# Trunk of retention, spatial gating and dilated attention: GpSimd's sums of weights begun earlier, probabilities and retention's output a tile later

## The chip, the cores and the metric

One core of a Trainium2 chip runs the whole program. TensorE (PE) multiplies, VectorE (DVE) and ScalarE (ACT) work on its results, GpSimd (POOL) and SyncE (SP) issue transfers; each engine works through its own list of instructions in order and waits on semaphores. The metric is the device time of one execution in microseconds; the median of three runs counts.

## What is computed

Two layers over 512 positions of width 1024. The reference, cut to what matters here:

```python
for l in range(DEPTH):                      # DEPTH = 2
    h = rms_norm(x, g_mix[l])
    z = h @ w_in[l]                         # q, k, v of all mixers and the branch gates
    # A: retention, 4 heads (rotation, decayed causal scores, head norm, swish gate)
    # B: spatial gating in chunks of 128
    # C: dilated attention, 4 heads x 3 groups; q and k are RMS-normalized per head
    for gi, (win, dil) in enumerate(((128, 1), (512, 4), (2048, 16))):
        o, lse = dilated_window_attention(qc[:, :, gi], kc[:, :, gi], vc[:, :, gi], win, dil)
    wts = jax.nn.softmax(jnp.stack(lses, axis=0), axis=0)   # weights of the three groups
    yc = jnp.sum(wts[..., None] * jnp.stack(outs, axis=0), axis=0)
    merged = (gt[:, :, 0] * (ya @ w_branch[l, 0])           # gt = sigmoid of the branch gates
              + gt[:, :, 1] * (yb @ w_branch[l, 1]) + gt[:, :, 2] * (yc @ w_branch[l, 2]))
    x = x + merged @ w_o[l]
    h = rms_norm(x, g_ffn[l])
    gate, up = jnp.split(h @ w_gate_up[l], 2, axis=-1)
    x = x + (silu(gate) * up) @ w_down[l]
```

## The kernel before

Everything is kept transposed, 128 channels by 512 positions. The weights come from DRAM in slabs of eight 128x128 blocks (512 KB): SP loads a slab into one of three `raw` buffers (L712), ACT rounds it to `w_high` (L1011, "split_high") and DVE takes the rest, `w_low` (L1215, "split_low"), into one of three places. A main tile is one output of 128 channels: eight blocks, three matmuls each (high by high, low by high, high by low), 24 matmuls of 512 columns. Its bank is evacuated by DVE, and the main tile after the next one takes that bank again.

`schedule()` writes one list of steps, and every engine walks the list and takes its part of each step. For each main tile the list has, in this order: the main matmuls; the high split of the slab that takes the place just used (so ACT waits there until PE has finished the tile); the steps in `pre` of that tile; the evacuation; the low split; the steps in `post`. So a step moved by one tile moves behind a whole main tile on PE, and behind another split on ACT.

The tiles of a head h of the attention are k0 k1 k2 q0 q1 q2 v0 v1 v2; after the fourth head come rq rk rv rg for each of retention's four heads, then the gates and projections of branch 2, and so on. The attention of a head is worked off beside the next head's projections (t is the number of the head's tile k0, so t + 9 is the next head's k0):

- `scores`, `expo`: scores in PSUM, DVE adds the mask and takes row maxima, ACT's exponentials with their sums (L1179).
- `gather`, `swap`: DVE writes the maxima and sums of own groups into `pairs` (L1477); SP sends them through DRAM and back (L750 to L760), so that each position meets its other order.
- `weigh`: DVE makes `shift` from own and exchanged pairs (L1483 to L1485), ACT takes `shift_exp` (L1184), DVE makes the factors and scales all probabilities (L1488 to L1500).
- `ptrans`: PE turns four units of probabilities (L949) into the two turn banks, 4 and 5, by turns; ACT copies them out (L1190). Every user of a turn bank (also `vtrans`, L931, and `rowstat`) waits until the user before the last has been copied or read.
- `pv`: values by probabilities, in bank 6. `high`/`low yc`: ACT and DVE split the result.
- For the next head at the same time: `square` and `split_sq` of k and q (L1101, L1108, L1430), `rowstat ck` (PE sums squares over channels with ones_r), `rowstd` (ACT's square root, L1117), `rowinv` (DVE's reciprocal, L1434), `rowscale`; `stat cq`, PE's column statistic of the squared q (`ones,sq`, eight matmuls of one column).
- Retention: `rotate`, `rscore`, `rpv`, `ocopy` of the output, the same square, statistic and reciprocal, `rowscale` and the split of yr.

An activation other than copy and square needs its table in ACT; where two in a row need different ones, the program has an ACT_TABLE_LOAD between them.

The feed-forward part multiplies seven products of quarters for nine of its eleven pairs of tiles ("quick"), and four of the seven need sums of weights, t1 to t4. POOL makes these in DRAM with eight transfers of 512 KB for each pair, four of them adding (L673, L675), each step waiting for the one before. It starts when tile rv0 of the layer has been stored. SP waits for a pair's eight before it loads its first sum.

Of the kernel before, what the change touches and what calls it, by code (L numbers as in the profile page):

```python
# [33 lines left out]
HEADS = 4  # L34
# [6 lines left out]
PAIRS = D_FF // P // 2  # L41
# [57 lines left out]
A11B11, S2T2, A12B21, S1T1, S3T3, S4B22, A22T4 = range(7)  # L99
# [4 lines left out]
AT = {t: i for i, t in enumerate(TILES)}  # L104
# [14 lines left out]
STRIDE = 16 * SLABS  # L119
# [74 lines left out]
def schedule():  # L194
    pre = {i: [] for i in range(len(TILES))}
    post = {i: [] for i in range(len(TILES))}
    for h in range(HEADS):
        t = AT["k", h, 0]
        for j in range(N_GROUP):

            post[t + j] += [("square", "ck", h, j), ("split_sq", "ck", h, j)]

            pre[t + (2, 4, 4)[j]] += [("rowstat", "ck", h, j), ("rowstd", "ck", h, j)]
            post[t + 3 + j] += [("rowinv", "ck", h, j), ("rowscale", "ck", h, j)]

            post[t + 3 + j] += [("square", "cq", h, j)]
            pre[t + 4 + j] += [("stat", "cq", h, j)]
            if j > 0:
                pre[t + 7 + j] += [("vtrans", "v", h, j)]
        pre[t + 6] += [("rstd", "cq", h)]  # L210
        pre[t + 7] += [("scores", h, 0), ("scores", h, 1), ("expo", h, 0), ("vtrans", "v", h, 0)]
        pre[t + 8] += [("scores", h, 2), ("scores", h, 3), ("expo", h, 1)]
        post[t + 8] += [("gather", h), ("swap", h)]
        if h < HEADS - 1:
            pre[t + 11] += [("weigh", h)]
        pre[t + 12] += [("ptrans", h, 0), ("ptrans", h, 1)]
        pre[t + 13] += [("ptrans", h, 2), ("pv", h, 0), ("ptrans", h, 3)]
        pre[t + 14] += [("pv", h, 1), ("pv", h, 2), ("high", "yc", h), ("low", "yc", h)]
    for h in range(HEADS):
        t = AT["rq", h]  # L220
        post[t] += [("rotate", "rq", h)]
        if h == 0:

            pre[t + 2] += [("weigh", HEADS - 1)]
        post[t + 1] += [("rotate", "rk", h)]
        pre[t + 3] += [("vtrans", "rv", h)] + [("rscore", h, m) for m in range(2)]
        pre[t + 4] += [("rscore", h, m) for m in range(2, BLK)]
        pre[t + 6] += [("rpv", h), ("ocopy", h), ("square", "r", h), ("split_sq", "r", h)]
        pre[t + 7] += [("rowstat", "r", h), ("rowstd", "r", h)]
        post[t + 7] += [("rowinv", "r", h)]  # L230
        post[t + 8] += [("rowscale", "r", h), ("high", "yr", h), ("low", "yr", h)]
    t = AT["sv", 0]
    for c in range(HEADS):
        pre[t + c + 1] += [("vtrans", "sv", c)]
# [64 lines left out]
STAT_AT, BCAST_AT = 3, 6  # L299
AFTER_NORM = (AT["k", 0, 0], AT["fgate", 0, 0])  # L300
STEPS = schedule()


# [46 lines left out]
def build(nc, x_in, weights, sums_dram, gain_first, vecs, spatial, rows, rotation, decay, masks, ident_in, pairs_dram, out):  # L350
    with ExitStack() as ctx:  # L351
# [3 lines left out]
        def signal(name, events, ahead=()):  # L355
            return Signal(ctx.enter_context(nc.semaphore(name)), events, ahead)
# [110 lines left out]
        tile_stored = signal("tile_stored", BY_VECTOR)  # L467
# [200 lines left out]
        def _(pool):  # L668
# [7 lines left out]
                started[0] += 1  # L676

            for layer in range(DEPTH):
                pool.wait_ge(tile_stored.sem, tile_stored.at(layer * STRIDE, AT["rv", 0]))
                for n, u in enumerate(QUICK_UNITS):  # L680
                    first = AT["quick", u, 0]
                    b11, b21, b22 = (weights[layer * HOST_ROWS + SOURCE[BLOCKS[first + step][0][0]]]
# [522 lines left out]
        def _(dve):  # L1205
# [26 lines left out]
            for base in range(0, DEPTH * STRIDE, STRIDE):  # L1232
# [23 lines left out]
                for kind, *key in STEPS:  # L1256
# [24 lines left out]
                    elif kind == "evac":  # L1281
# [41 lines left out]
                        elif t[0] in ("q", "k"):  # L1323
                            operands = by_phase(qk[t[2] + (3 if t[0] == "k" else 0)], src, norm_rstd[:, :], t[2] > 0)
                            dve.tensor_tensor(*operands, ALU.mult).then_inc(tile_stored.sem, 1)
                        elif t[0] == "proj":
                            _, br, n = t
                            dve.wait_ge(activated.sem, activated.at(base, AT["gate", br, n]))
                            g = gates[GATE_TILES.index(AT["gate", br, n]) % 2]
# [331 lines left out]
```

## Time and profile before

| what | value |
|---|---|
| median of three runs | 1927.08 us (1926.92 to 1927.63) |
| profiled execution, its own time | 1928.07 us |
| its span | 1926.3 us |
| PE busy | 1902.9 us |
| DVE busy | 1236.6 us |
| ACT busy | 854.4 us |
| POOL busy (issuing) | 97.0 us |
| TensorE's granted clock, mean | 0.999 |
| ACT_TABLE_LOADs (six lines together) | 49 |

The span is from the first instruction of the program to the last. PE's matmuls overlap in the records: a matmul of 512 columns is shown with 0.38 us, but starts 0.22 us after the one before it, so starts are to be compared, not ends. The time in brackets at the end of a row is idle time of its engine and what ended it.

### The profile page before, as it was taken

To read this page: it belongs to the slowest core of one execution; us is meant where nothing else is said; L and a number is where in the kernel's file an instruction comes from. 1 tells how busy PE (TensorE), PEld (TensorE's weight loads), DVE (VectorE), ACT (ScalarE), POOL (GpSimd) and SP (SyncE) were. 2 spreads that over 40 slices of the span, in tenths; PEclk is the share of its full clock that TensorE was granted. 3 is DMA by queue.
4 is the path that set the end of the run, shared out by engine and by line. 5 is a ranking of instruction groups with operands and counts; after the bars stand their busy time and mean duration, and the time that the engine had idled before them with its cause. 6 is when DMAs were issued, how large, how long until landed. Compare 5 with 4: busy or idle time off the path is not lost. (4 is left out here: it accounts for less than half of the span.)

```text
span 1926.3 us, 26698 instructions
## 1 busy us (share of the span) xinstructions
PE 1902.9 (99%) x10664; PEld 1703.1 (88%) x10664; DVE 1236.6 (64%) x1633; ACT 854.4 (44%) x1194; POOL 97.0 (5%) x148
## 2 busy tenths in 40 slices
PE   7999999999999999999999999999999999999999
PEld 6888888888888899899888888888888888998998
DVE  6666756745666787267576666677366667863775
ACT  5444444434234455255445444344343344542554
POOL 0000001111111000000000000011111110000000
PEclk9999999999999999999999999999999999999999
DMA  5322247777777356356333222577777773553663
GB/s 190 83 81 84 78 121 197 192 207 202 214 206 198 99 158 182 102 183 198 122 108 87 74 78 79 138 198 188 216 193 199 200 206 106 176 157 109 204 204 126
DMA packets 85897, 295.68 MB, mean 153 GB/s; under 512 B 20368, under 2 KB 20624, under 8 KB 84624
## 3 DMA queue, kind: packets, MB, share of 16 engines
q1 hardware_dynamic: 73104, 218.49, 36.4%
q0 software_dynamic: 12672, 75.51, 17.3%
q8 instruction: 85, 1.39, 0.3%
q14 instruction: 36, 0.29, 0.1%
HBM read 291.79 MB, written 77.66 MB: 192 GB/s over the span
## 5 line engine op out<-in xcount | busy, mean ns | idle before, releaser
L1011 ACT ACTIVATE w_high<-raw 128x1024 fp32r<-128x1024 f32 x396 | 418.1, 1056 | 813.3 <-PE bank L823 685.7
L823 PE MATMUL bank<-h_high,w_high 128*128 128x512 f32 x1472 | 570.1, 387 | 12.8 <-DVE h_low L1220 11.3
L1215 DVE TENSOR_TENSOR w_low<-raw,w_high 128x1024 fp32r<-128x1024 f32 x396 | 482.8, 1221 | 123.3 <-ACT w_high L1011 117.5
L823 PE MATMUL bank<-h_low,w_high 128*128 128x512 f32 x1472 | 559.2, 380 | 0.0
L823 PE MATMUL bank<-h_high,w_low 128*128 128x512 f32 x1472 | 559.1, 380 | 0.0
L823 PEld LDWEIGHTS bank<-h_high,w_high 128*128 128x128 f32 x1472 | 279.2, 190 | 55.9 <-issue 9.4
L823 PEld LDWEIGHTS bank<-h_high,w_low 128*128 128x128 f32 x1472 | 279.0, 190 | 39.8
L823 PEld LDWEIGHTS bank<-h_low,w_high 128*128 128x128 f32 x1472 | 279.2, 190 | 38.3
L823 PE MATMUL bank<-in_high,w_high 128*128 128x512 f32 x672 | 255.0, 379 | 0.0
L823 PE MATMUL bank<-in_low,w_high 128*128 128x512 f32 x672 | 254.7, 379 | 0.0
L823 PE MATMUL bank<-in_high,w_low 128*128 128x512 f32 x672 | 254.7, 379 | 0.0
L1322 DVE TENSOR_TENSOR scaled<-bank,norm_rstd 128x512 f32<-128x512 f32 x128 | 93.7, 732 | 108.3 <-PE bank L823 107.8
L841 PE MATMUL bank<-s_high,w_high 128*128 128x256 f32 x576 | 158.4, 275 | 0.0
L842 PE MATMUL bank<-s_low,w_high 128*128 128x256 f32 x576 | 158.4, 275 | 0.0
L843 PE MATMUL bank<-s_high,w_low 128*128 128x256 f32 x576 | 158.4, 275 | 0.0
L823 PEld LDWEIGHTS bank<-in_high,w_high 128*128 128x128 f32 x672 | 127.0, 189 | 18.3 <-DVE in_low L1413 0.4
L823 PEld LDWEIGHTS bank<-in_high,w_low 128*128 128x128 f32 x672 | 127.0, 189 | 18.0
L823 PEld LDWEIGHTS bank<-in_low,w_high 128*128 128x128 f32 x672 | 127.0, 189 | 17.8
L843 PEld LDWEIGHTS bank<-s_high,w_low 128*128 128x128 f32 x576 | 110.6, 192 | 0.0
L842 PEld LDWEIGHTS bank<-s_low,w_high 128*128 128x128 f32 x576 | 110.6, 192 | 0.0
L841 PEld LDWEIGHTS bank<-s_high,w_high 128*128 128x128 f32 x576 | 110.6, 192 | 0.0
L1345 DVE TENSOR_TENSOR xT<-bank,xT 128x512 f32<-128x512 f32 x32 | 22.1, 691 | 125.3 <-PE bank L823 125.3
(156 smaller groups left out, 2253.1 us busy)
## 6 DMA issues: line engine op xcount, KB each, us to landing
raw<-weights SPq DMA_DIRECT2D x325, 512.0 KB, 4.0
weight_sums<-weights POOLq DMA_DIRECT2D x108, 512.0 KB, 6.1
raw<-weight_sums SPq DMA_DIRECT2D x72, 512.0 KB, 3.5
weight_sums<-weight_sums POOLq DMA_DIRECT2D x36, 512.0 KB, 4.0
turned<-rows SPq DMA_DIRECT2D x3, 768.0 KB, 7.0
xT<-x_t SPq DMA_DIRECT2D x8, 256.0 KB, 5.6
decay_sb<-decay SPq DMA_DIRECT2D x8, 256.0 KB, 4.5
out_t<-xT SPq DMA_DIRECT2D x8, 256.0 KB, 6.4
```

Source lines behind the costliest of these rows:

```text
L823: return pe.matmul(o, w, m, start=start, stop=stop)
L841: pe.matmul(part, wh, hi, start=k + c == 0 and not onto, stop=False, skip_group_check=onto)
L842: pe.matmul(part, wh, lo, start=False, stop=False, skip_group_check=onto)
L843: last = pe.matmul(part, wl, hi, start=False, stop=k == 3 and c == 1, skip_group_check=onto)
L1011: act.activation(w_high[:, PART_SLOT[s], :, :], raw[:, s % RAW_SLOTS, :, :], ACT.Copy).then_inc(part_high_w.sem, 1)
L1215: dve.tensor_tensor(w_low[:, PART_SLOT[s], :, :], raw[:, s % RAW_SLOTS, :, :], w_high[:, PART_SLOT[s], :, :], ALU.subtract).then_inc(part_ ...
L1322: dve.tensor_tensor(*operands, ALU.mult).then_inc(tile_stored.sem, 1)
L1345: dve.tensor_tensor(x, src.rearrange("p (t a i) -> p i a t", a=2, i=2), x, ALU.add).then_inc(tile_stored.sem, 1)
```

## The change

Three things, all in the order of work; no computation changes.

- `weigh`, `ptrans`, `pv` and the split of yc come one tile later for all four heads of the attention.
- `rpv` and all that follows it (output copy, squares, statistic, reciprocal, scaling, split of yr) come one tile later for the four heads of retention. `rscore` and `vtrans` of retention stay.
- POOL begins the first layer's sums when the third tile of the program (k2 of the first head) is stored, and the second layer's when the last product of the first layer's quick part is stored, before the second half of its down projection.

```diff
         if h < HEADS - 1:
-            pre[t + 11] += [("weigh", h)]
-        pre[t + 12] += [("ptrans", h, 0), ("ptrans", h, 1)]
-        pre[t + 13] += [("ptrans", h, 2), ("pv", h, 0), ("ptrans", h, 3)]
-        pre[t + 14] += [("pv", h, 1), ("pv", h, 2), ("high", "yc", h), ("low", "yc", h)]
+            pre[t + 12] += [("weigh", h)]
+        pre[t + 13] += [("ptrans", h, 0), ("ptrans", h, 1)]
+        pre[t + 14] += [("ptrans", h, 2), ("pv", h, 0), ("ptrans", h, 3)]
+        pre[t + 15] += [("pv", h, 1), ("pv", h, 2), ("high", "yc", h), ("low", "yc", h)]
     for h in range(HEADS):
         t = AT["rq", h]
         post[t] += [("rotate", "rq", h)]
         if h == 0:
 
-            pre[t + 2] += [("weigh", HEADS - 1)]
+            pre[t + 3] += [("weigh", HEADS - 1)]
         post[t + 1] += [("rotate", "rk", h)]
         pre[t + 3] += [("vtrans", "rv", h)] + [("rscore", h, m) for m in range(2)]
         pre[t + 4] += [("rscore", h, m) for m in range(2, BLK)]
-        pre[t + 6] += [("rpv", h), ("ocopy", h), ("square", "r", h), ("split_sq", "r", h)]
-        pre[t + 7] += [("rowstat", "r", h), ("rowstd", "r", h)]
-        post[t + 7] += [("rowinv", "r", h)]
-        post[t + 8] += [("rowscale", "r", h), ("high", "yr", h), ("low", "yr", h)]
+        pre[t + 7] += [("rpv", h), ("ocopy", h), ("square", "r", h), ("split_sq", "r", h)]
+        pre[t + 8] += [("rowstat", "r", h), ("rowstd", "r", h)]
+        post[t + 8] += [("rowinv", "r", h)]
+        post[t + 9] += [("rowscale", "r", h), ("high", "yr", h), ("low", "yr", h)]
...
             for layer in range(DEPTH):
-                pool.wait_ge(tile_stored.sem, tile_stored.at(layer * STRIDE, AT["rv", 0]))
+                if layer == 0:
+                    pool.wait_ge(tile_stored.sem, tile_stored.at(0, AT["k", 0, 2]))
+                else:
+                    pool.wait_ge(tile_stored.sem, tile_stored.at(0, AT["quick", PAIRS - 1, A22T4]))
```

What this does to ACT's list beside the fourth head's projections of the first layer, where the third head is weighed. The rows run from the split behind tile k2 to the copies of the first two units of probabilities. Before:

```order
L1011 ACTIVATE w_high<-raw 128x1024
L1184 ACTIVATE shift_exp<-shift 128x16
L1117 ACT_TABLE_LOAD
L1117 ACTIVATE prod<-bank,eps 128x512
L1101 ACTIVATE sq<-work 128x512
L1108 ACTIVATE in_high<-work 128x512
L1011 ACTIVATE w_high<-raw 128x1024
L1190 ACTIVATE work<-bank 128x384
L1190 ACTIVATE work<-bank 128x512
L1101 ACTIVATE sq<-work 128x512
```

After, with every line number of these three higher:

```order
L1014 ACTIVATE w_high<-raw 128x1024
L1120 ACT_TABLE_LOAD
L1120 ACTIVATE prod<-bank,eps 128x512
L1104 ACTIVATE sq<-work 128x512
L1111 ACTIVATE in_high<-work 128x512
L1014 ACTIVATE w_high<-raw 128x1024
L1187 ACT_TABLE_LOAD
L1187 ACTIVATE shift_exp<-shift 128x16
L1104 ACTIVATE sq<-work 128x512
L1014 ACTIVATE w_high<-raw 128x1024
L1193 ACTIVATE work<-bank 128x384
L1193 ACTIVATE work<-bank 128x512
```

`shift_exp` has moved from behind the split of tile k2 to behind that of tile q0, past the square root, and has a table load of its own; the last `sq` of q0 now stands before the copies. A third table load follows these rows, before the square root of k1. In the whole list ACT has 59 table loads, where it had 49.

PE's list behind tile q0 and tile q1 of the same head (the 24 matmuls of q1 are left out). Before:

```order
L949 MATMUL bank4<-identity,work 128x128 x3
L949 MATMUL bank5<-identity,work 128x128 x4
...
L949 MATMUL bank4<-identity,work 128x128 x4
L823 MATMUL bank6<-work 128x128 x7
L949 MATMUL bank5<-identity,work 128x128 x4
L823 MATMUL bank7<-ones,sq 128x1 x4
L823 MATMUL bank4<-in_high,ones_r 128x512
L823 MATMUL bank4<-in_low,ones_r 128x512
```

After, behind tile q1 alone (behind q0 nothing stands):

```order
L952 MATMUL bank4<-identity,work 128x128 x3
L952 MATMUL bank5<-identity,work 128x128 x4
L826 MATMUL bank7<-ones,sq 128x1 x4
L826 MATMUL bank4<-in_high,ones_r 128x512
L826 MATMUL bank4<-in_low,ones_r 128x512
L826 MATMUL bank5<-in_high,ones_r 128x512
```

The first row statistic, which takes bank 4, now stands two short steps behind the first unit of probabilities in bank 4, where three units and a `pv` lay between them.

PE's list behind tile rg0, where the fourth head's probabilities meet retention's first values. Before:

```order
L949 MATMUL bank5<-identity,work 128x128 x3
L949 MATMUL bank4<-identity,work 128x128 x4
L931 MATMUL bank5<-identity,scaled 128x128 x4
L823 MATMUL bank2<-work 128x512
L823 MATMUL bank3<-work 128x384
```

After, behind rg0 and then, after the 24 matmuls of the next tile, behind rq1:

```order
L934 MATMUL bank5<-identity,scaled 128x128 x4
L826 MATMUL bank2<-work 128x512
L826 MATMUL bank3<-work 128x384
...
L952 MATMUL bank4<-identity,work 128x128 x3
L952 MATMUL bank5<-identity,work 128x128 x4
L826 MATMUL bank2<-work 128x256
L826 MATMUL bank3<-work 128x128
```

The turned values no longer follow the probabilities into a bank that is still being copied.

## Rows read from the trace of the kernel before

**Rows 1.** The page: engine, busy time, share of the span, instructions.

```profile
PE 1902.9 (99%) x10664; PEld 1703.1 (88%) x10664; DVE 1236.6 (64%) x1633; ACT 854.4 (44%) x1194; POOL 97.0 (5%) x148
```

**Rows 2.** Waits of PE: who waited for whom, total, times, longest.

```profile
PE bank L823 <- DVE h_low L1220: 11.3, 5, 8.7
```

**Rows 3.** PE in order of time, third head: start, duration, work [idle before].

```profile
209.19 0.40 PE L823 MATMUL bank<-in_high,ones_r 128*128 128x512 f32 x1
...
209.66 0.38 PE L823 MATMUL bank<-h_high,w_high 128*128 128x512 f32 x1
...
214.84 0.93 PE L949 MATMUL bank<-identity,work 128*128 128x128 f32 x7
215.52 0.46 PE L823 MATMUL bank<-h_high,w_high 128*128 128x512 f32 x1
...
223.22 0.95 PE L823 MATMUL bank<-ones,sq 128*128 128x1 f32 x8
224.03 0.48 PE L823 MATMUL bank<-in_high,ones_r 128*128 128x512 f32 x1
...
224.57 0.39 PE L823 MATMUL bank<-in_high,ones_r 128*128 128x512 f32 x1
```

**Rows 4.** PE in order of time, behind tile rg0 of the first layer.

```profile
274.67 0.93 PE L949 MATMUL bank<-identity,work 128*128 128x128 f32 x7
276.42 0.66 PE L931 MATMUL bank<-identity,scaled 128*128 128x128 f32 x4 [0.82 <-ACT work L1190]
```

**Rows 5.** PE in order of time, retention's last row statistic, first layer.

```profile
378.62 0.38 PE L823 MATMUL bank<-in_high,w_low 128*128 128x512 f32 x1
379.16 0.47 PE L823 MATMUL bank<-in_high,ones_r 128*128 128x512 f32 x1 [0.15 <-DVE in_low L1430]
```

**Rows 6.** ACT in order of time, third head.

```profile
209.45 1.06 ACT L1011 ACTIVATE w_high<-raw 128x1024 fp32r<-128x1024 f32 x1 [2.91 <-PE bank L823]
210.41 0.20 ACT L1184 ACTIVATE shift_exp<-shift 128x16 f32<-128x16 f32 x1
210.63 1.28 ACT L1117 ACT_TABLE_LOAD   x1
211.93 0.69 ACT L1117 ACTIVATE prod<-bank,eps 128x512 f32<-128x512 f32 x1
214.92 0.63 ACT L1101 ACTIVATE sq<-work 128x512 f32<-128x512 f32 x1 [2.31 <-DVE work L1325]
215.46 0.61 ACT L1108 ACTIVATE in_high<-work 128x512 fp32r<-128x512 f32 x1
215.98 1.04 ACT L1011 ACTIVATE w_high<-raw 128x1024 fp32r<-128x1024 f32 x1
216.92 0.96 ACT L1190 ACTIVATE work<-bank 128x384 f32<-128x384 f32 x2
```

**Rows 7.** DVE in order of time, third head.

```profile
198.89 0.17 DVE L1477 TENSOR_TENSOR pairs<-den 128x4 f32<-128x4 f32 x1 [1.94 <-ACT work L1179]
...
207.18 0.16 DVE L1483 TENSOR_TENSOR shift<-pairs 128x8 f32<-128x8 f32 x1
...
212.56 1.29 DVE L1500 TENSOR_TENSOR work<-work,factor 128x512 f32<-128x512 f32 x2
213.77 1.06 DVE L1325 TENSOR_TENSOR work<-bank,norm_rstd 128x512 f32<-128x512 f32 x1
...
216.71 0.68 DVE L1325 TENSOR_TENSOR work<-bank,norm_rstd 128x512 f32<-128x512 f32 x1
```

**Rows 8.** Weight loads (L712), issue to landing: 30 to 265 us, then 280 to 615.

```profile
DMA to landing us min/median/max: 3.5/3.6/6.1
...
DMA to landing us min/median/max: 3.3/4.6/8.3
```

**Rows 9.** Last transfer of the first layer's sums, and the first load of one.

```profile
614.51 0.81 POOL L673 DMA_DIRECT2D weight_sums<-weights  x1 [3.73 <-DMA weight_sums<-weight_sums]
...
664.85 0.33 SPq L712 DMA_DIRECT2D raw<-weight_sums  x1
```

## The prediction

> **What bounds the kernel now.** I read four views, in this order. The page's table of busy time says that PE, TensorE's matmuls, is busy 1902.9 of 1926.3 us [rows 1]. So the end moves only by what PE itself waits for, and a change that moves work between engines can bring little and can cost more. The view of PE's waits says where the few idle microseconds are: 11.3 of them are for h_low at the very start, which this change does not touch [rows 2]. Two waits that it does touch are visible in PE's order of time. In the fourth head the turned probabilities are followed at once by the transposition of retention's values, and that one starts 1.75 us after the first instead of 0.68 [rows 3, 4]; both layers have it. After the last rpv, the statistic for retention's output starts 0.54 us after the matmul before it, where two main matmuls stand 0.22 apart [rows 5]. The page's releasers say ACT's copy and DVE's in_low.
>
> The last step was to ask how close the other engines are to becoming PE's limit around the moved steps. Take the third head (the fourth's keys and queries are being projected). PE finishes tile k2 at 209.19 and starts its next tile, q0, at 209.66 [rows 3]. ACT starts that tile's weight split at 209.45, the exponential for the weights of the softmax groups at 210.41, then loads another activation table for 1.28 us and takes a square root [rows 6]. DVE, which begins on shift at 207.18, can scale the probabilities only behind that exponential, and ends at 212.56 + 1.29 = 213.85 [rows 7]. PE takes the probabilities at 214.84 [rows 3]: one microsecond to spare in a chain that looks idle. The exponential did not wait for the exchange of the pairs through DRAM (sent from 198.9, used at 207.18, 8.3 us) but for PE, because in ACT's order it stands behind a split that waits for PE to finish a tile [rows 6, 7].
>
> **The sums of weights, by themselves: 0.** GpSimd issues its last transfer of the first layer at 614.51 and SP the first load of a sum at 664.85 [rows 9], so 50 us lie between them, and PE does not wait for a sum. Beginning them 36 tiles earlier saves nothing. What they do is move traffic into the attention. A weight load beside the sums takes 4.6 us in the middle where one in the first attention takes 3.6, and 8.3 at most against 6.1 [rows 8]. The loads are issued some two tiles ahead there, so I price this at 0 and keep one late load, 8.3 - 3.6 = 4.7 us, as the bound above. A bound below zero has no ground, as nothing on PE waits for these loads where the sums now stand.
>
> **Fourth head and retention: a gain of 2.8 us.** The fourth head's probabilities move a tile away from the transposition of retention's values, so the 1.75 - 0.68 = 1.07 us go, twice: 2.14. What is late next there? weigh(3) is prepared in tile rg0 behind one split and no new table. By the offsets above it ends 213.85 - 209.19 = 4.66 us after PE has finished that tile, and PE comes back for it after one whole tile, 214.84 - 209.66 = 5.18 us, at the soonest. It is hidden by 0.5 us or more. The statistic after the last rpv now stands behind a gate tile of 5.18 instead of a short projection, so 0.54 - 0.22 = 0.32 us go, twice: 0.64. DVE's reciprocal moves one tile on for each head and now precedes a rotation; the evacuation behind it has two tiles of time, so 0. ACT saves one table load per layer there, off the path, 0.
>
> **The other three heads: a loss, and the core of the forecast.** Before, the weigh exponential of these heads followed other exponentials in the ACT order, and the square root came after it. One tile later it stands behind that square root, and the next square root behind it. The order of the changed kernel has a table load in front of the exponential and another in front of the next square root: ten more loads in all, two for each of the six heads and one fewer per layer in retention. The first of the two lies in the chain. Count from M, the time at which PE finishes tile q0:
>
> 1. The split starts at M + 0.26 (209.45 against 209.19) and ends 1.06 later, at M + 1.32 [rows 3, 6]. A table load starts 0.02 behind its forerunner, takes 1.28, and its follower starts 0.02 behind it (210.41 + 0.20 = 210.61, 210.63, 211.91, 211.93). Exponential: M + 2.64, where it was M + 1.22.
> 2. From exponential to probabilities is 213.85 - 210.41 = 3.44 [rows 6, 7]. Scaled: M + 6.08. PE wants them at M + 5.18. With 0.09 to pass the signal (DVE's evacuation ends at 213.77 + 1.06 = 214.83, ACT goes on at 214.92), PE starts at M + 6.17, and **0.99 us** are lost.
> 3. DVE evacuates q0 only behind weigh: M + 6.00 to M + 6.68 (0.68) [rows 7]. ACT squares it 0.09 later for 0.63: M + 7.40. The column statistic that PE wants after its two transpositions (6.17 + 0.68 = 6.85) must wait to M + 7.49: **0.64 us**. Before, it stood a tile later, with that square long done.
> 4. ACT goes from that square to the next split (at + 0.54) and from the split to the copies of the probabilities (216.92 - 215.98 = 0.94): copies at M + 8.25. The first lasts some 0.48 and both together 0.96, so bank 4 is free at M + 8.73. PE's row statistic, which in the new order takes this bank, could start at 7.49 + 0.81 = M + 8.30 and starts at M + 8.82: **0.52 us**. The other bank is free to PE at M + 9.30, just before the second statistic (8.82 + 0.54 = 9.36) [rows 3, 6].
>
> Together 0.99 + 0.64 + 0.52 = 2.15 us per head, six times: 12.9. Behind these steps PE has whole tiles again. DVE comes to its reciprocal (L1434) later than before, but the next tile's evacuation is done some 7 us behind that of q0 by my estimate, near M + 13, and PE needs it two tiles on, near M + 18, so nothing more is added.
>
> A rule speaks on step 1. The rows show 1.28 us for a load and the next instruction 0.02 us behind it [rows 6]. The Trainium skill, "ScalarE: Activation LUTs", section "What ACT_TABLE_LOAD costs", gives about 1283 ns for the load and about 1380 ns of drain besides, 2.66 us for every switch. By that the trace agrees with the first figure and not with the second, and the sum would be larger by six times 1.38.
>
> **The sum.** 12.9 - 2.14 - 0.64 = +10.1 us on PE. Span: 1926.3 + 10.1 = 1936.4. The profiled execution was 1928.1 with 1.8 outside its span, so 1938.2; the median of the three timed runs is 1927.1, 1.0 below it, so 1937.2.
>
> **Rivals.**
> *The table load does not bind.* If ACT could place it in the idle time before the split, or if the exponential were no later for it, weigh would end at M + 4.66 as now, before PE comes. Then steps 2 and 3 shrink to nearly nothing. The copies would start at M + 5.18 + 1.22 = M + 6.40, behind the next tile's split, and let PE have the bank at 6.40 + 0.48 + 0.09 = 6.97, where it wants it at 5.18 + 0.68 + 0.81 = 6.67: 0.30 us, six times 1.8. Time: 1927.1 + 1.8 - 2.8 = 1926.1, not slower. For it: the square at steps 3 and 4 is the only other late thing. Against it: the order has the load behind the split, and the load at 210.63 began only when its forerunner ended [rows 6]. 0.13, with the half-way cases that stay below 3.9 us.
> *GpSimd's traffic holds up the exchange of pairs.* It crosses DRAM twice and is used 8.3 us after it was sent. After the change it is used by the exponential at M + 2.64, that is 214.84 + 2.64 = 217.48, or 18.6 us behind 198.89: room for 10.3 more. A large load beside the sums took 1.0 more in the middle and 4.7 more (8.3 against 3.6) at most [rows 8]; for two legs 2 to 9.4, which still fits. It decides only from 10.3 on. A head at twice the middle of that range, 11.4, would lose 1.1, all six 6.6; one weight load at its worst would lose up to 4.7. I price the case at +6: 1943. The Trainium skill, "DMA: Bandwidth & Descriptors", section "Queues, rings and completion order", says that an engine takes whole packets from its queues in turn, which would let small packets wait for GpSimd's large ones; no run of before shows the two side by side. 0.11.
> *The drain of the page's rule is real behind an exponential.* Then each of the six loads in the chain costs 1.38 more: 1937.2 + 8.3 = 1945.5. The rows at 210.63 and 211.93 speak against it. 0.02. It is the result that the Trainium skill's page on activation tables, named above, would give.
> *A gain over 3.9 us.* The waits that the change can remove are 2.8 us in all. 0.02, for something that no row shows.
>
> **How the numbers follow.** The forecast, 1937.2, has 0.72, with 1932 to 1942 as its own width: every one of the three waits is a difference of two chains some 6 us long. Two runs of this kernel differ by so little that 0.2%, 3.9 us, is about what a measurement can tell from no change. With the first rival's time at 1926 and its half-way cases just above it, and the traffic case at 1943, the range for 8 in 10 is 1930 to 1944. Faster 0.02; same 0.14 (first rival and the lowest edge of the forecast); slower 0.84.
>
> **What would show it.** In the changed profile: 59 table loads instead of 49, and one of them at the weigh exponential in six heads; in those heads PE idle before its transpositions of probabilities (near 1 us), before the statistic of squares (near 0.6) and before the row statistic (near 0.5); no wait before the transposition of retention's values nor before the last row statistic; the sums ended by 400 us. I am wrong if PE has no wait before the probabilities there, if shift (DVE) and not the exponential is what ends late, or if waits for weight loads appear beside the sums.

## The result and the profile after

| | before | after |
|---|---|---|
| median of the timed runs, us | 1927.31 (1926.92 to 1927.63, 4 runs) | 1944.76 (1943.46 to 1945.78, 4 runs) |
| profiled execution, us | 1928.1 | 1945.78 |
| its span, us | 1926.3 | 1944.0 |
| mean granted clock of its span | 0.999 | 0.996 |

The ratio is 1.0091, with a 95% interval of 1.0076 to 1.0106. The change costs 17.4 us where 10.1 were forecast, and the time lies 0.8 us above the range.

The page of the changed kernel: engine, busy time, share of the span, instructions. It answers to [rows 1].

```profile
PE 1911.9 (98%) x10664; PEld 1707.4 (88%) x10664; DVE 1236.3 (64%) x1633; ACT 868.1 (45%) x1204; POOL 97.3 (5%) x148
```

ACT has ten instructions more, 1204 for 1194, and is 13.7 us longer busy: the ten table loads. PE has the same 10664 matmuls and is 9.0 us longer busy, which waits alone would not do. That is the first sign of a slower clock.

Who PE waited for, in total, how often, and the longest (view of the waits):

```profile
PE bank L826 <- DVE h_low L1223: 10.0, 3, 8.1
PE bank L952 <- DVE work L1503: 4.8, 6, 0.8
...
PE bank L826 <- ACT sq L1104: 2.6, 6, 0.4
PE bank L826 <- DVE work L1334: 2.5, 2, 1.2
...
PE bank L826 <- ACT work L1193: 1.3, 6, 0.2
```

The lines that stand six times are the three waits of the forecast: for the probabilities, for the square of q0, and for the copies that free bank 4. Their totals are idle time in the records, in which matmuls are shown with overlapping ends; counted between starts, as the forecast counts, the three are longer (below). The waits of the fourth head for ACT's copy and of the last row statistic for in_low [rows 4, 5] are gone. L1334 is a wait of which the forecast says nothing.

The first of the six heads, PE in order of time (start, duration, work, [idle before]); this answers to [rows 3]. Here M, the end of PE's tile q0, is 93.52.

```profile
98.48 0.38 PE L826 MATMUL bank<-h_high,w_low 128*128 128x512 f32 x1
99.66 0.98 PE L952 MATMUL bank<-identity,work 128*128 128x128 f32 x7 [0.79 <-DVE work L1503]
101.07 1.02 PE L826 MATMUL bank<-ones,sq 128*128 128x1 f32 x8 [0.43 <-ACT sq L1104]
102.30 0.50 PE L826 MATMUL bank<-in_high,ones_r 128*128 128x512 f32 x1 [0.21 <-ACT work L1193]
```

ACT of the same stretch, as in [rows 6]:

```profile
93.78 1.06 ACT L1014 ACTIVATE w_high<-raw 128x1024 fp32r<-128x1024 f32 x1 [1.55 <-PE bank L826]
94.86 1.28 ACT L1187 ACT_TABLE_LOAD   x1
96.15 0.21 ACT L1187 ACTIVATE shift_exp<-shift 128x16 f32<-128x16 f32 x1
100.30 0.63 ACT L1104 ACTIVATE sq<-work 128x512 f32<-128x512 f32 x1 [3.93 <-DVE work L1328]
100.83 1.04 ACT L1014 ACTIVATE w_high<-raw 128x1024 fp32r<-128x1024 f32 x1
101.78 0.96 ACT L1193 ACTIVATE work<-bank 128x384 f32<-128x384 f32 x2
```

And DVE, as in [rows 7]:

```profile
92.87 0.16 DVE L1486 TENSOR_TENSOR shift<-pairs 128x8 f32<-128x8 f32 x1
...
98.31 1.29 DVE L1503 TENSOR_TENSOR work<-work,factor 128x512 f32<-128x512 f32 x2
99.52 0.68 DVE L1328 TENSOR_TENSOR work<-bank,norm_rstd 128x512 f32<-128x512 f32 x1
```

PE starts on the probabilities at M + 6.14, where it wanted them at 5.18. From there to the statistic 1.41 us pass instead of 0.68, and from the statistic to the row statistic 1.23 instead of 0.81. Counted so, between starts and with the forecast's step lengths, the three waits are 0.96, 0.73 and 0.42 us, 2.11 in all. (The expectations below, written before, put the last two at 0.59 and 0.35.)

The load begins 0.02 us behind the split and the exponential 0.01 behind the load. shift was begun at 92.87, some 3 us before the exponential, so the exchange does not set the end of this chain; the load, behind a split that waits for PE, does.

What the forecast did not have is in the view by stretches. Columns: stretch, its length, then busy time of PE, PEld, DVE, ACT and POOL, granted clock, busy share of the DMA engines, GB/s. The first three rows are the first head (the waits, and what follows them), the last two the same steps of the second head.

```profile
99.60:102.70 3.10, 2.41 (x17) 2.01 (x17) 3.10 (x3) 2.40 (x4) 0.52 (x1) 1.00 0.47 151
102.70:106.10 3.40, 3.40 (x10) 2.64 (x9) 3.37 (x3) 2.59 (x4) 0.81 (x1) 0.51 0.43 174
106.10:110.00 3.90, 3.90 (x20) 3.42 (x19) 3.90 (x3) 0.64 (x1) 0.00 (x0) 0.99 0.92 176
163.60:166.70 3.10, 2.41 (x17) 2.01 (x17) 3.10 (x3) 2.41 (x4) 0.52 (x1) 1.00 0.38 62
166.70:170.00 3.30, 3.30 (x17) 2.80 (x16) 3.27 (x3) 2.58 (x4) 0.00 (x0) 1.00 0.81 303
```

For 3.4 us behind the three waits the granted clock is 0.5, the 1.2 GHz level, and PE starts only 10 matmuls; then it is back at 2.4 GHz. In the second head, with the same three waits (0.80, 0.43, 0.21 us), it stays at 2.4 GHz. The records of the attention show four such stretches, from about 102.7, 229.0, 1065.2 and 1191.6 us: the first and the third head of each layer. The kernel before has none there.

**Where the time went**, between starts of the same tiles of PE, in us:

| stretch | before | after | difference |
|---|---|---|---|
| start to tile k2 of the first head | 27.97 | 27.27 | -0.7 |
| tile q0 of the second head to tile rg0, layer 1 | 180.46 | 189.92 | +9.46 |
| the same, layer 2 | 180.46 | 189.85 | +9.39 |
| rg0 to past the end of retention, layer 1 | 136.18 | 136.16 | 0 |
| the same, layer 2 | 136.17 | 136.18 | 0 |
| all the rest | 1265.04 | 1264.61 | -0.4 |

Within the second and third row, q0 and the two tiles behind it take 25.06 us where the clock falls and 23.45 where it does not: 1.61 us for each fall. Four of them are 6.4 us, and 18.85 - 6.4 = 12.4 are the waits of six heads, 2.07 each. The fourth and fifth row are a balance of zero that hides three terms: -1.07 and -0.32, the two gains of the forecast, and +1.41 for the wait at L1334. The first row is no effect of the change: kernels below begin their first k2 between 26.7 and 28.1 us.

### The profile page after: what moved, and what is told of

Read it like the earlier page. It is cut to its first block and busy times, and to the rows that moved or that the text cites. A ratio compares the mean times of both kernels' runs of the same rounds, so it can differ in the third digit from the quotient of the medians.

```text
span 1944.0 us, 26708 instructions
## 1 busy us (share of the span) xinstructions
PE 1911.9 (98%) x10664; PEld 1707.4 (88%) x10664; DVE 1236.3 (64%) x1633; ACT 868.1 (45%) x1204; POOL 97.3 (5%) x148
## 3 DMA queue, kind: packets, MB, share of 16 engines
q0 software_dynamic: 12672, 75.51, 17.4%
```

## The experiments

The kernel before ran beside each; its median was 1926.8 to 1927.0. Numbers without a unit are us.

**The two halves of the change apart.** First only GpSimd's start is taken over:

```diff
--- the kernel before
-                pool.wait_ge(tile_stored.sem, tile_stored.at(layer * STRIDE, AT["rv", 0]))
+                if layer == 0:
+                    pool.wait_ge(tile_stored.sem, tile_stored.at(0, AT["k", 0, 2]))
+                else:
+                    pool.wait_ge(tile_stored.sem, tile_stored.at(0, AT["quick", PAIRS - 1, A22T4]))
```

> The kernel before with GpSimd's sums begun early and no step moved. In the changed kernel the exchange of pairs took 13 to 15 us in several heads (gather at 77.57, shift at 92.87) where it took 8.3 before. In this kernel the exponential stands one tile earlier, about 10.3 us behind the gather, so where the exchange takes 14 us the probabilities come some 3 to 4 us late and PE waits. Theory (traffic stretches the exchange of small packets, and the move of the probabilities covers that): PE waits before the probabilities in most of the 8 heads, 1 to 5 us each, about 1940 in all (1932 to 1955), with further half-clock stretches. Rival (traffic by itself costs nothing, as the prediction had it): 1927, no wait before the probabilities.

Measured: 1948.84 (1938.86 to 1956.01, 4 runs), ratio 1.0109 [1.0072, 1.0146]. By itself the early start of the sums, for which the forecast has 0, costs 22 us. The four runs lie far apart, so the 22 is rough. Waits of PE, DVE where it waits for the exchange, PE behind that, and the transfers from 30 to 265 us, the attention of the first layer (issues, size, median us to landing):

```profile
PE bank L952 <- DVE work L1503: 17.3, 7, 4.2
```

```profile
93.32 0.17 DVE L1486 TENSOR_TENSOR shift<-pairs 128x8 f32<-128x8 f32 x1 [7.92 <-DMA pairs<-pairs_by_token]
```

```profile
97.31 1.75 PE L952 MATMUL bank<-identity,work 128*128 128x128 f32 x7 [4.17 <-DVE work L1503]
```

```profile
weight_sums<-weights POOLq DMA_DIRECT2D x36, 512.0 KB, 5.9
raw<-weights SPq DMA_DIRECT2D x34, 512.0 KB, 4.5
weight_sums<-weight_sums POOLq DMA_DIRECT2D x12, 512.0 KB, 4.4
pairs_by_token<-pairs SPq DMA_DIRECT2D x6, 4.0 KB, 7.1
pairs<-pairs_by_token SPq DMA_DIRECT2D x6, 4.0 KB, 3.6
```

The same view of the kernel before:

```profile
raw<-weights SPq DMA_DIRECT2D x36, 512.0 KB, 3.6
pairs_by_token<-pairs SPq DMA_DIRECT2D x8, 4.0 KB, 4.9
pairs<-pairs_by_token SPq DMA_DIRECT2D x6, 4.0 KB, 2.3
```

A transfer of 4 KB takes 7.1 us in the middle beside those of 512 KB, where it took 4.9, and its way back 3.6 instead of 2.3. In the head shown the way out takes 10.0. From gather to shift 16.3 us pass there (77.03 to 93.32) instead of 8.3 [rows 7], and in the old order the probabilities are wanted sooner than that. The seven waits sum to 17.3, of which the kernel before has 1.6 in another form. The granted clock is at 0.5 for 17.1 us in all. That costs at most half of it, 8.5, since a part of the slow time lies in the waits themselves: in the head shown the clock is down from about 95.6, and PE starts at 97.31. Together at most 24.2, and the span grew by 24.7. The Trainium skill, "DMA: Bandwidth & Descriptors", section "Queues, rings and completion order", says that an engine drains a whole packet of one queue before it turns to the next; the two views agree with that, though they cannot show the packets' turns themselves.

Then the order of the changed kernel with GpSimd's start as before (the same lines, the other way):

> The changed kernel with GpSimd's sums begun where they were before. Theory (the loss comes from the order: table load and exponential behind a split, then half clock after the waits): the same three waits of 0.96, 0.59 and 0.35 us in six heads, the same wait of 1.41 near retention's last head, and some stretches at half clock: 1942 to 1946. Rival (the early traffic has a large part in the loss, or brings the clock down): 1935 or less, and no stretch at half clock in the attention.

Measured: 1942.67 (1942.03 to 1944.87, 4 runs), ratio 1.0083 [1.0067, 1.01]. The three waits are the same to 0.1 us (4.8, 2.6, 1.3), so they come from the order and not from the traffic. This run's span is 3.3 below that of the changed kernel, and its attention has two stretches at 1.2 GHz (from 164.5 in the second head and 1188.5 in the last of the six) where that has four: twice 1.61 is 3.2. Whether the traffic makes such stretches more frequent is not shown: the mean clocks of the timed runs are 0.996 to 0.998 in both kernels. The order costs 15.8 us without the early sums and 17.4 with them, while the early sums cost 22 in the old order. So the later move covers most of what the traffic does to the exchange, at a price of its own.

**The table load.** The square root in front of the exponential is replaced in the three heads by a square, which needs no other table. This leaves the root out, so the results are not those of the reference; only the time is read, as that of a schedule with two loads less in each of the six heads:

```diff
--- the changed kernel
-                                       turn_bank[...][:, :], ACT.Sqrt,
+                                       turn_bank[...][:, :],
+                                       ACT.Square if key[0] == "ck" and key[1] > 0 and key[2] == 0 else ACT.Sqrt,
```

> The changed kernel, but the first row statistic of k in heads 1 to 3 is squared by ACT instead of having its square root taken, so that no table has to be loaded before the exponential of weigh nor for this step: this leaves out the square root, and the time is to be read as that of a schedule with 12 table loads less. Theory (the load in the chain makes the probabilities late): the probabilities end about 1.3 us sooner, PE does not wait for them; the waits for the square and for the copy shrink from 0.94 to about 0.8 us per head; without long idle stretches the clock stays full: 1944.8 - 6 x 1.1 - 6.8 = about 1931 (1929 to 1934). Rival (the exponential is late for another reason, say DVE's backlog or the exchange): 1944, waits unchanged.

Measured: 1930.93 (1930.35 to 1932.38, 10 runs), ratio 1.0021 [1.0012, 1.003]. 47 table loads for 59, and 13.8 us less than the changed kernel. PE waits for:

```profile
PE bank L826 <- DVE work L1335: 2.5, 2, 1.2
PE bank L918 <- DVE rs L1430: 2.0, 2, 1.2
...
PE bank L826 <- ACT work L1194: 1.2, 6, 0.2
```

No wait before the probabilities, a single one of 0.3 for the square where there were six, and no stretch at 1.2 GHz in the attention. The order of PE's work is that of the changed kernel, so the order of PE's work by itself costs 4.2 us in the six heads; what costs most is where the change sends ACT's loads. The wait that went with it is 0.96, close to the 0.99 that step 2 gives for a load of 1.28 alone, and the row at 96.15 has the exponential 0.01 behind the load: the drain that the Trainium skill, "ScalarE: Activation LUTs", section "What ACT_TABLE_LOAD costs", adds to each switch was not there. What is left over the kernel before in this span, 4.2, is 4.2 in the six heads (0.19 and 0.42 at each one's two statistics, the rest in slower first matmuls behind them) and 1.5 at the start of the second layer, less 1.4 at start and end; retention's three terms cancel here too. The 1.5 are behind a weight load that lands late there (ACT waits 1.78 for it), once in this run and not in the changed kernel's.

**The new wait at the last retention head.** Only that head's `rpv` and what follows it go back by a tile:

```diff
--- the changed kernel
-        pre[t + 7] += [("rpv", h), ("ocopy", h), ("square", "r", h), ("split_sq", "r", h)]
-        pre[t + 8] += [("rowstat", "r", h), ("rowstd", "r", h)]
+        e = 6 if h == HEADS - 1 else 7
+        pre[t + e] += [("rpv", h), ("ocopy", h), ("square", "r", h), ("split_sq", "r", h)]
+        pre[t + e + 1] += [("rowstat", "r", h), ("rowstd", "r", h)]
...
-        post[t + 9] += [("rowscale", "r", h), ("high", "yr", h), ("low", "yr", h)]
+        post[t + e + 2] += [("rowscale", "r", h), ("high", "yr", h), ("low", "yr", h)]
```

> The changed kernel with the output of retention's last head (rpv, statistic, reciprocal, scaling) put back by one tile, the other heads as changed. Theory (DVE's reciprocal and scaling of the last head now run into two short projections, and the evacuation that PE needs is late by 1.41 us): that wait goes in both layers and the 0.32 us before the row statistic come back, so 2.2 us less, about 1942.6, to be read best from PE's waits. Rival (the wait comes from ACT's sigmoid or from weight traffic): the 1.41 us stay.

Measured: 1941.52 (1940.16 to 1947.61, 4 runs), ratio 1.0081 [1.0065, 1.0097]. The line on L1334 is gone from PE's waits, and the small one of before is back:

```profile
PE bank L827 <- DVE in_low L1434: 0.3, 2, 0.2
```

So the wait belongs to this move. The changed kernel shows how. DVE in order of time, with PE's wait as the last line:

```profile
395.07 3.35 DVE L1437 RECIPROCAL work<-work 128x512 f32<-128x512 f32 x1 [0.78 <-ACT work L1120]
398.46 0.69 DVE L1325 TENSOR_TENSOR scaled<-bank,norm_rstd 128x512 f32<-128x512 f32 x1
399.07 1.22 DVE L1218 TENSOR_TENSOR w_low<-raw,w_high 128x1024 fp32r<-128x1024 f32 x1
400.20 0.75 DVE L1448 SCALAR_TENSOR_TENSOR tmp<-work,vec 128x512 f32<-128x512 f32 x1
400.98 0.69 DVE L1450 TENSOR_TENSOR prod<-tmp,work 128x512 f32<-128x512 f32 x1
402.61 0.69 DVE L1416 TENSOR_TENSOR in_low<-prod,in_high 128x512 fp32r<-128x512 f32 x1 [0.94 <-ACT in_high L1154]
403.22 1.28 DVE L1334 TENSOR_TENSOR work<-bank,work 128x512 f32<-128x512 f32 x2
```

```profile
403.96 0.48 PE L826 MATMUL bank<-h_high,w_high 128*128 128x512 f32 x1 [1.25 <-DVE work L1334]
```

The reciprocal and the scaling chain behind it now stand ahead of the evacuations of two projection tiles. PE works on one of those for only 2.59 us (397.37 to 399.96), not 5.18, and wants the first one's bank again at once. The median fell by 3.2. Of that, 2.8 less the returned 0.6 are this move; the remaining 1.0 is less than one fall of the clock costs, and the profiled execution has two falls in the attention, at 227.2 and 1124.9, where the changed kernel has four.

**The clock.** PE gets something to do while it waits: six, three and two matmuls of 384 columns into a spare bank, before the probabilities, the statistic and the row statistic. Nobody reads what they write.

```diff
--- the changed kernel
+            def fill(n):
+                for _ in range(n):
+                    matmul(stat_bank[:, P:SEQ], ones_r[:, :], h_high[:, 0, 0:SEQ - P], True, True)
...
                         h, u = key
+                        if u == 0 and h < HEADS - 1:
+                            fill(6)
                         pe.wait_ge(probs_ready.sem, probs_ready.at(base, h))
...
+                    if key[1] > 0 and key[2] == 0:
+                        fill(3)
                     pe.wait_ge(squared.sem, squared.at(base, *key))
...
+                        if key[0] == "ck" and key[1] > 0 and key[2] == 1:
+                            fill(2)
                         o = turn(base, (kind,) + key)
```

> The changed kernel with matmuls that nobody reads, put in front of the three waits of heads 1 to 3: 6, 3 and 2 matmuls of 384 columns (0.16 us each) into columns of bank 7 that hold nothing. They fill the 0.96, 0.59 and 0.35 us in which PE stood idle; the probabilities come no sooner. Theory (TensorE's clock falls to half after these waits, and costs 1.7 us in each of the two to four heads where it does): no stretch at half clock in the attention, the work waited for at the same times, so 1944.8 - 3.4 to 6.8 = 1938 to 1941, and a smaller spread between runs. Rival (the half-clock stretches come with the time or the load, not with the waits): still two to four of them, 1945.

Measured: 1939.87 (1939.47 to 1940.22, 4 runs), ratio 1.0067 [1.0053, 1.0081]. With 66 matmuls more it is 4.9 faster than the changed kernel, and the span is 6.2 shorter, near the 6.4 of four falls. From tile q0 of the second head to tile rg0 it takes 186.67 us in either layer: 6.21 more than the kernel before, and 3.25 and 3.18 less than the changed one. So 12.4 us belong to the six heads at the full clock, 2.07 each, and 6.4 to the clock. No stretch of the attention is at 1.2 GHz. The first head, by stretches, this kernel and then the changed one:

```profile
98.00:104.00 6.00, 6.00 (x38) 5.29 (x37) 6.00 (x6) 3.46 (x5) 0.81 (x1) 1.00 0.66 126
```

```profile
98.00:104.00 6.00, 4.57 (x24) 3.43 (x24) 6.00 (x6) 3.69 (x5) 0.52 (x1) 0.90 0.37 114
104.00:110.00 6.00, 6.00 (x25) 5.04 (x24) 5.96 (x5) 1.95 (x4) 0.81 (x1) 0.82 0.78 188
```

PE idles 1.43 us of the first six in the changed kernel and none here. This is the direct evidence that the waits cost more than their length: what they added through the clock is 4.9 in the median and 6.4 in the profiled execution.

**Only the gains.** The kernel before with the fourth head's probabilities a tile later, and retention's first `rpv` with what follows it; the other heads and GpSimd as before:

```diff
--- the kernel before
-        pre[t + 12] += [("ptrans", h, 0), ("ptrans", h, 1)]
+        e = 1 if h == HEADS - 1 else 0
+        pre[t + 12 + e] += [("ptrans", h, 0), ("ptrans", h, 1)]
...
-            pre[t + 2] += [("weigh", HEADS - 1)]
+            pre[t + 3] += [("weigh", HEADS - 1)]
...
-        pre[t + 6] += [("rpv", h), ("ocopy", h), ("square", "r", h), ("split_sq", "r", h)]
+        e = 7 if h == 0 else 6
+        pre[t + e] += [("rpv", h), ("ocopy", h), ("square", "r", h), ("split_sq", "r", h)]
```

> The kernel before with only the fourth head's weigh, probabilities and pv a tile later, and with them the output of retention's first head (so that it does not wait for yc). Sums and the first three heads as before. Theory (the 1.07 us before retention's turned values go in both layers and nothing becomes late, as weigh of this head has no table load before its exponential): 1927.1 - 2.1 = 1925.0, no new wait on PE. Rival (what is saved there comes back as another wait, in retention or at a bank): 1927 or more.

Measured: 1924.58 (1924.41 to 1925.20, 11 runs), ratio 0.9988 [0.9979, 0.9997]. The forecast's 2.14 for this step is 2.4 here, and 2.1 from rg0 to past the end of retention in the two layers of the profiled execution.

The next one adds the last row statistic, a tile later, but lets its scaling come only behind the projections' evacuations, so that no wait is put in its place:

```diff
--- the kernel above
-        e = 7 if h == 0 else 6
+        e = 7 if h in (0, HEADS - 1) else 6
...
-        post[t + e + 2] += [("rowscale", "r", h), ("high", "yr", h), ("low", "yr", h)]
+        post[t + e + (5 if h == HEADS - 1 else 2)] += [("rowscale", "r", h), ("high", "yr", h), ("low", "yr", h)]
```

> The kernel of the fourth head alone, and besides the output of retention's last head a tile later with its scaling put behind the short projections (four tiles on). Theory: the 0.32 us before the last row statistic go in both layers, and the 1.41 us that the changed kernel has at the projections do not come, since the scaling no longer precedes the evacuation that PE needs: 1925.0 - 0.6 = 1924.4. Rival (the reciprocal alone makes that evacuation late): a wait of about 1 us stays there, 1926.

Measured: 1923.60 (1923.35 to 1924.22, 11 runs), ratio 0.9982 [0.9974, 0.9991]. Neither the wait for in_low nor that of L1334 in the changed kernel is among PE's waits; from rg0 to past the end of retention the two layers take 3.0 less than before. It is the fastest kernel of this study, by 3.4 us on the kernel before and 21.2 on the changed one.

**Can the six heads keep the move without the load?** Here `weigh` of the first three heads goes back to its old place, ahead of the square root, while the transpositions of the probabilities stay a tile later:

```diff
--- the changed kernel
-            pre[t + 12] += [("weigh", h)]
+            pre[t + 11] += [("weigh", h)]
```

> The changed kernel with weigh of heads 0 to 2 back where it was, one tile ahead of the probabilities' transpositions by two, sums early. The exponential follows other exponentials again: no load before it. But the exchange beside the sums takes 13 to 16 us, and DVE waits for it with the evacuation of tile k2 behind, which PE needs 11.3 us after the gather or a little later. Theory: no wait before the probabilities, a wait of PE for that evacuation in most of the six heads, 0 to 6 us each depending on the exchange: 1930 to 1950, with a wide spread between runs. Rival (only the table load mattered): 1929 to 1931, narrow.

Measured: 1952.62 (1947.27 to 1958.75, 4 runs), ratio 1.0134 [1.0116, 1.0153]: no load in the chain, and yet 7.9 slower than the changed kernel. PE's waits, DVE ahead of one of them, and PE behind it:

```profile
PE bank L826 <- DVE work L1328: 15.6, 7, 4.5
PE bank L918 <- DVE rs L1429: 3.2, 2, 2.4
```

```profile
92.77 0.17 DVE L1486 TENSOR_TENSOR shift<-pairs 128x8 f32<-128x8 f32 x1 [7.30 <-DMA pairs<-pairs_by_token]
...
96.63 1.02 DVE L1328 TENSOR_TENSOR work<-bank,norm_rstd 128x512 f32<-128x512 f32 x1
```

```profile
97.71 0.79 PE L826 MATMUL bank<-h_high,w_high 128*128 128x512 f32 x1 [4.50 <-DVE work L1328]
```

PE no longer waits for the probabilities. It waits for a bank, because the evacuation of k2 stands behind shift and the scaling of the probabilities in DVE's list, and shift waits 7.3 us for the exchange. Whether it is the traffic that makes it late was the question of the next kernel, with the sums begun as before (the edit above and GpSimd's line of the kernel before):

> The changed kernel with weigh of heads 0 to 2 back by a tile (no table load before its exponential) and the sums begun where they were before: all that is left of the change is that probabilities and pv, and retention's output, come a tile later. Theory: no wait before the probabilities nor before the square's statistic; the row statistic still waits for ACT's copy of the probabilities, about 0.35 us in six heads (2.1 in all), and the 1.41 us near retention's last head stay: 1927.0 + 2.1 + 2.8 - 2.1 - 0.6 = 1929.2 (1928.5 to 1930). Rival (the 22 us of the same order with early sums are the order's own, not the exchange's): 1940 or more.

Measured: 1929.11 (1928.88 to 1929.56, 10 runs), ratio 1.0011 [1.0002, 1.002]. The same order with the early sums takes 23.5 us more. Without them the six heads take 2.5 us more than in the kernel before (181.85 and 181.56 us for 180.46 twice), near the 2.1 of the expectation. DVE waits 0.23 for the exchange instead of 7.30:

```profile
85.79 0.17 DVE L1483 TENSOR_TENSOR shift<-pairs 128x8 f32<-128x8 f32 x1 [0.23 <-DMA pairs<-pairs_by_token]
```

**The traffic in the changed order.** The filled kernel once more, with the sums begun as before, so that no fall of the clock blurs the comparison:

> The kernel with the filled waits, and GpSimd's sums begun where they were before. Both kernels with filled waits keep the full clock, so their difference is what the early traffic costs by itself in the changed order. Theory (the exchange is hidden by the order, only a late weight load at the start of the second layer remains): 0 to 2 us less than the 1939.9 with early sums, 1938 to 1939.9. Rival (the traffic costs more than waits show, on every weight load): 1936 or less.

Measured: 1939.01 (1938.78 to 1940.27, 4 runs), ratio 1.0062 [1.0045, 1.0078], against 1939.87. Where the exponential has a tile more, the early sums cost about 0.9, hardly more than the scatter: the two sets of runs overlap (1938.78 to 1940.27 and 1939.47 to 1940.22). From q0 of the second head to rg0 the two kernels agree to 0.03 us in either layer, so PE loses nothing to the traffic there.

## Why the prediction was right or wrong

**Right: steps 1 to 4, almost to the instruction.** Offsets from M in the first head, from the rows above:

| | forecast | measured |
|---|---|---|
| exponential starts (step 1) | 2.64 | 96.15 - 93.52 = 2.63 |
| probabilities scaled (step 2) | 6.08 | 98.31 + 1.29 - 93.52 = 6.08 |
| PE starts on them | 6.17 | 6.14 |
| square of q0 done (step 3) | 7.40 | 100.30 + 0.63 - 93.52 = 7.41 |
| column statistic | 7.49 | 7.55 |
| copies start (step 4) | 8.25 | 8.26 |
| row statistic | 8.82 | 8.78 |

The three waits are 0.96, 0.73 and 0.42 for 0.99, 0.64 and 0.52, so two small errors partly cancel. A head costs 2.07 instead of 2.15, six of them 12.4 instead of 12.9. The one-load experiment shows the cause and the order-only one that no traffic is needed for it.

**Right: the gains.** 2.14 and 0.64; the two kernels that make only these moves are 2.4 and 3.4 faster than the kernel before.

**Wrong: "so nothing more is added".** The sum counts each wait at its own length and has no term for TensorE's clock, which it leaves at 2.4 GHz. All of the forecast's durations came from stretches in which PE has no waits. But the trace of the kernel before has such a fall at its start, where PE waits 0.39, 1.48 and 0.39 us for h_low, from 14.3 to 18.4 us (stretches, columns as above):

```profile
16.00:19.00 3.00, 1.47 (x5) 1.02 (x6) 3.00 (x6) 2.53 (x4) 0.00 (x0) 0.96 0.33 133
19.00:22.00 3.00, 3.00 (x8) 2.37 (x8) 1.12 (x1) 0.00 (x0) 0.00 (x0) 0.50 0.76 203
```

A reader of these rows would have had a reason to leave room for the clock, though not its price in the heads. There, in four of six heads, behind three waits of 0.96, 0.73 and 0.42 us, it went to 1.2 GHz for 3.4 us, 1.61 each: 6.4 in the profiled execution, 4.9 in the median by the filled kernel. It is the largest part of the miss, and it made the range too narrow: the range took in the sizes of the waits, and nothing that grows out of them.

**Wrong: "the evacuation behind it has two tiles of time, so 0".** That holds where the tiles are of 5.18 us. Behind the last retention head they are projections of 2.59, and the reciprocal's chain now stands ahead of two evacuations. 1.41 in each layer, 2.8 in all: by chance just as much as the two gains.

**Half wrong: "the sums of weights, by themselves: 0".** In the changed order they cost 0.9 at most; in the order of before, which is what "by themselves" means, 22. The working looked at the room for weight loads and not at the small transfers of the exchange, although they are the ones with little time to spare there. The rival on that traffic had the mechanism and the room right: the exponential starts 18.6 us behind the gather (77.57 to 96.15). The exchange is slower and still fits. SP issues its way back at 88.7, 10.9 behind the way out, and in the order-only kernel 4.5 behind. Yet shift begins 15.3 behind the gather in both kernels, when DVE comes to it. The price of +6 did not arise.

**The rivals.** "The table load does not bind" fell with the row at 94.86. The drain that the Trainium skill, "ScalarE: Activation LUTs", section "What ACT_TABLE_LOAD costs", gives would have made it 1945.5. That this is near the measured time is luck: the exponential starts 0.01 us behind the load, and the missing time is in the clock and at L1334.

**The sum with the terms as measured:** 12.4 + 6.4 - 2.14 - 0.64 + 2.8 = 18.8 on PE, less 1.1 at the start and the end, which the change does not touch: 17.7, the growth of the span (1926.3 to 1944.0). In the medians the forecast missed 17.4 - 10.1 = 7.3: 4.9 for the clock and 2.8 for L1334, less 0.5 for waits that were a little shorter, make 7.2.

One thing stays open: why the clock falls in some heads and not in others, when the same three waits stand in all of them. It is not tied to the head. The changed kernel falls in the first and third of each layer, the order-only kernel in the second of the first layer and the third of the second, and the kernel with the last retention head put back in the third and then the second.

## What to carry to other kernels

When a step moves in an in-order list, look at what its new neighbours do to it: one square root passed over put a table load into a chain with one microsecond to spare, and without that load the changed kernel is 13.8 us faster. When you put a term at nothing, measure what covers it at every place where the step occurs, the last head with its short tiles included, and a new stream of large transfers has to be held against the smallest and most urgent transfer beside it, not against the large ones. And a new wait of TensorE can be worth more than its length where several stand close together; once the waits are forecast, leave room for the clock in the range.

## What the runs showed of the hardware

- The granted clock of TensorE went from 2.4 to 1.2 GHz behind waits each shorter than 1 us, 0.51 over 3.4 us, and came back by itself, in four of the six heads that have these waits. With waits of 0.2 and 0.4 us a head (one load less), or with dummy matmuls in them, it did not fall. The clock's two levels are those of the Trainium skill, "TensorE: Matmul & The Clock Gate", section "Part 1: The HAM clock gate".
- A 4 KB transfer, issued from SP, took 7.1 us beside GpSimd's transfers of 512 KB and 4.9 without; its return leg 3.6 instead of 2.3; the loads of 512 KB 4.5 instead of 3.6 (medians, 30 to 265 us, sums only against before). In proportion the small ones suffered most; one pair of them took 10.0.
- A table load took 1.28 us in all 59 cases of the changed kernel. In 41 the next instruction came 0.01 to 0.02 behind it, and in the other 18 it waited for its input.
